# Dilated layer of a two-layer transformer trunk: query/key tiles of two of its three dilations transposed by DMA instead of TensorE

## The reference

```
DIL_PATTERNS = ((128, 1), (512, 4), (2048, 16))       # window, dilation

def dilated_mixer(a, cos, sin, w_in, w_o):
    proj = (a @ w_in).reshape(B, S, N_DIL, 3, H, DH)   # S = 256, H = 16 heads, DH = 64
    outs, lses = [], []
    for gi, (window, dil) in enumerate(DIL_PATTERNS):
        q = partial_rope(proj[:, :, gi, 0], cos, sin)
        k = partial_rope(proj[:, :, gi, 1], cos, sin)
        v = proj[:, :, gi, 2]
        o, lse = banded_attention(to_residue(q, dil)[:, :, :, None], to_residue(k, dil),
                                  to_residue(v, dil), window // dil)
        outs.append(from_residue(o[:, :, :, 0], B, dil))
        lses.append(from_residue(lse[:, :, :, 0], B, dil))
    alpha = jax.nn.softmax(jnp.stack(lses, axis=-1), axis=-1)
    o = jnp.einsum('bshn,bshnd->bshd', alpha.astype(a.dtype), jnp.stack(outs, axis=3))
    return o.reshape(B, S, H * DH) @ w_o
```

## Time and profile before

| | |
|---|---|
| median of 3 runs | 810.8 us (810.62 to 811.05) |
| the profiled execution, its own time | 810.76 us |
| its span, first to last instruction | 809.0 us |
| mean granted TensorE clock | 0.997 |
| PE busy / DVE busy / ACT busy / POOL busy | 798.6 / 528.5 / 457.5 / 102.2 us |
| the dilated layer in the trace | about 342 to 618 us |

### The profile page before, as it was taken

The page is one execution under the profiler, slowest core; times in us unless marked ns, Lnnn a source line. Parts: engine busy times, 40 slices in busy tenths (PEclk is TensorE's granted clock), DMA queues, the critical chain, the costliest instruction groups (busy, mean ns, idle before and its releaser), DMA issues.

```text
span 809.0 us, 11869 instructions
## 1 busy us (share of the span) xinstructions
PE 798.6 (99%) x4401; PEld 643.8 (80%) x4401; DVE 528.5 (65%) x1121; ACT 457.5 (57%) x879; POOL 102.2 (13%) x167
## 2 busy tenths in 40 slices
PE   9999999999999999999999999999999999999996
PEld 7877675788888888788888888888877888888885
DVE  6966969796565556697566665766668775655644
ACT  7836877765444444575555566555658554444431
POOL 1000005812212221000000000000000112222210
PEclk9999999999999999999999999999999999999998
DMA  9955211168886687658544535363424688678811
GB/s 318 351 184 200 86 54 53 59 189 241 242 212 191 191 238 216 188 198 269 157 157 153 160 121 192 105 208 105 157 88 172 191 248 224 173 197 236 236 21 52
DMA packets 128490, 142.24 MB, mean 176 GB/s; under 512 B 25856, under 2 KB 111920, under 8 KB 128304
## 3 DMA queue, kind: packets, MB, share of 16 engines
q1 hardware_dynamic: 107760, 132.53, 52.6%
q10 hardware_dynamic: 19680, 4.75, 3.6%
q0 software_dynamic: 992, 4.19, 1.4%
HBM read 134.64 MB, written 2.10 MB: 169 GB/s over the span
## 4 chain that ended last, share of the span: by engine, by line
PE 96%; DVE 2%; ACT 1%; issue 0%; POOL 0%; ACTq 0%; POOLq 0%
PE ps L1830 86%; PE ps L1839 6%; PE ps L2107 2%; PE ps L2080 2%; PE ps L2118 1%; PE ps L1892 1%; ACT junk L756 0%; DVE w_lo L1256 0%; ACT xd_hi L744 0%; ACT w_hi L735 0%; ACT probs_b L907 0%; DVE h L1580 0%; DVE h L1586 0%; DVE tmp L1584 0%; ACT p_t L922 0%
## 5 line engine op out<-in xcount | busy, mean ns | idle before, releaser
L1256 DVE TENSOR_TENSOR w_lo<-w_raw,w_hi 128x1024 fp32r<-128x1024 f32 x240 | 295.5, 1259 | 64.8 <-ACT w_hi L735 62.5
L735 ACT ACTIVATE w_hi<-w_raw 128x1024 fp32r<-128x1024 f32 x240 | 245.5, 1060 | 3.0 <-DMA w_raw<-in_ffn_w_gu 2.9
L1830 PE MATMUL ps<-w_hi,xt_hi 128*128 128x512 f32 x472 | 188.5, 401 | 0.3 <-ACT w_hi L735 0.3
L1830 PE MATMUL ps<-w_hi,xt_lo 128*128 128x512 f32 x472 | 183.5, 390 | 0.0
L1830 PE MATMUL ps<-w_lo,xt_hi 128*128 128x512 f32 x472 | 183.0, 390 | 0.0
L1830 PE MATMUL ps<-w_hi,xd_hi 128*128 128x512 f32 x288 | 117.4, 408 | 0.2 <-DVE w_lo L1256 0.2
L1830 PE MATMUL ps<-w_hi,xd_lo 128*128 128x512 f32 x288 | 113.2, 393 | 0.0
L1830 PE MATMUL ps<-w_lo,xd_hi 128*128 128x512 f32 x288 | 112.8, 392 | 0.0
L1830 PEld LDWEIGHTS ps<-w_hi,xt_hi 128*128 128x128 f32 x472 | 88.5, 188 | 25.0 <-issue 8.6
L1830 PEld LDWEIGHTS ps<-w_hi,xt_lo 128*128 128x128 f32 x472 | 88.6, 188 | 18.9
L1830 PEld LDWEIGHTS ps<-w_lo,xt_hi 128*128 128x128 f32 x472 | 88.7, 188 | 16.7 <-DVE w_lo L1256 0.3
(11 more groups left out here) (271 smaller groups left out, 984.9 us busy)
## 6 DMA issues: line engine op xcount, KB each, us to landing
w_raw<-in_ffn_w_gu SPq DMA_DIRECT2D x88, 512.0 KB, 5.6
w_raw<-in_dil_w_in SPq DMA_DIRECT2D x72, 512.0 KB, 4.6
w_raw<-in_ffn_w_down SPq DMA_DIRECT2D x44, 512.0 KB, 5.4
w_raw<-in_nsa_w_in SPq DMA_DIRECT2D x20, 512.0 KB, 7.3
w_raw<-in_nsa_w_o SPq DMA_DIRECT2D x8, 512.0 KB, 4.8
w_raw<-in_dil_w_o SPq DMA_DIRECT2D x8, 512.0 KB, 4.5
w_k<-in_nsa_cmp_wk SPq DMA_DIRECT2D x2, 1024.0 KB, 9.0
w_raw<-in_nsa_cmp_wv SPq DMA_DIRECT2D x2, 1024.0 KB, 11.5
```

The lines of the kernel that those rows point to most:

```text
L735: act.activation(w_hi[:, n.slot, c:c + 1024], w_raw[:, n.slot, c:c + 1024], ACT.Copy)\
L1256: dve.tensor_tensor(w_lo[:, n.slot, c:c + 1024], w_raw[:, n.slot, c:c + 1024], w_hi[:, n.slot, c:c + 1024].bitcast(F32), ALU.subtract)\
L1830: ins = pe.matmul(o, s, m, start=start, stop=stop, **kw)
```

## The change

Patterns 1 and 2 no longer go through PE. Their 16 tiles (four in each group, `BARS`) take the way of the FFN's hidden tiles: POOL splits `stage_dil` into planes (`split_qk`, 1024 columns of 16 bits), ACT issues a DMA transpose of them (`dil_planes`), POOL merges them into `qk_t` in class order (`merge_qk`, four copies of 256 elements a partition, six where pattern 2 has m = 0). The planes lie in the place of `h`, two buffers of each. So POOL saves `h` in two parts, ahead of its first split, and reads it back after the last merge. Every group now has the order 1, 2, 0: pattern 0 last, still turned on PE (`PE_TURNS`, 8 tiles). The factor -1/8 of the queries moves from the copies to the mask operation. PE's scores wait for the merges, do the parts of patterns 1 and 2 first, and then wait for `qk_lo`.

```diff
 def qk_order(g):
-    return (1, 2, 0) if g == 0 else (1, 0, 2)
+    return (1, 2, 0)
...
+BARS = [x for x in TILES if x.kind == QK and x.pat]
+PE_TURNS = [x for x in TILES if x.kind == QK and not x.pat]
...
+            def split_qk(x):
+                pool.wait_ge(roped[1], x.qk_no + 1)
+                pool.tensor_copy(view(planes_q, BARS.index(x) % 2 * 1024, [[512, 2], [1, 512]]),
+                                 halves_of(stage_dil[:, x.qk_no % 2, :])).then_inc(planes_ready, 1)
...
+            def merge_qk(x):
+                i, pos = BARS.index(x), qk_order(x.g).index(x.pat)
+                pool.wait_ge(planes_turned[i % 2], 16 * (xbar_of(0, FJ - 2, i % 2) + i // 2 + 1))
+                if x.g - (pos == 0) > 0:
+                    pool.wait_ge(scores[1], 8 * (x.g - (pos == 0)))
...
+                for plane in range(2):
+                    q = at + plane + 2 * 32 * x.m
+                    pool.tensor_copy(u16_at(whole, q, [[2 * S, 2], [2 * P, 2], [2 * 64, 2], [2, 32]]),
+                                     view(planes_qt, src + 512 * plane, [[P, 2], [1, 2], [2, 2], [4, 32]]))
...
+                    ins = pool.tensor_copy(u16_at(whole, k - 2 * shift, [[2 * S, 2], [2 * P, 2], [2, 64 - first]]),
+                                           view(planes_qt, k_src + 2 * first, [[P, 2], [1, 2], [2, 64 - first]]))
+                ins.then_inc(ht_merged, 1)
...
-                    pool.dma_start(h_rows.rearrange("(m p) c -> p m c", m=MT), h[:, :, :]).then_inc(h_saved, 16)
+                    save_h(0)
                     pool.wait_ge(h_saved, 16)
+                    save_h(1)
...
+                    for g in range(DIL_G):
+                        first, second, third, fourth = [x for x in BARS if x.g == g]
+                        split_qk(first)
+                        split_qk(second)
+                        merge_qk(first)
+                        split_qk(third)
+                        merge_qk(second)
+                        split_qk(fourth)
+                        merge_qk(third)
+                        merge_qk(fourth)
+                    pool.wait_ge(ht_merged, len(XBAR) + DIL_BARS)
                     pool.dma_start(h[:, :, :], h_rows.rearrange("(p m) c -> p m c", m=MT)).then_inc(h_permuted, 16)
...
+            def dil_planes(x):
+                if x not in BARS:
+                    return
+                i = BARS.index(x)
+                if i == 0:
+                    act.wait_ge(h_saved, 16 * MT)
...
+                act.wait_ge(planes_ready, bar_at(x) + 1)
+                act.dma_start_transpose(planes_qt[:, i % 2, :, :], planes_q[:, i % 2, :])\
+                   .then_inc(planes_turned[i % 2], 16)
...
-            dil_turn_out(TILES[0])
             dil_evac(TILES[1])
             h_squares(2, 1)
             split(n + 1)
             split(n + 2)
-            dil_turn_out(TILES[1])
+            dil_planes(TILES[0])
+            dil_planes(TILES[1])
             dil_evac(TILES[2])
             split(n + 3)
-            dil_turn_out(TILES[2])
+            dil_planes(TILES[2])
             for e in range(4, LAST_E):
...
                 dil_evac(TILES[e - 1])
...
                     split(n + k, (1,))
+                dil_planes(TILES[e - 1])
                 dil_turn_out(TILES[e - 1])
...
             def dil_turn(x):
-                if x.kind != QK:
+                if x not in PE_TURNS:
                     return
```

More of the change, by code:

```diff
@@ L119, with bar_at @@
 XBAR = [(1, 0), (1, 1)] + [(j, m) for j in range(2, FJ - 1) for m in range(MT)]
+DIL_BARS = 2 * MT * DIL_G
 def xbar_no(layer, j, m):
-    return len(XBAR) * layer + XBAR.index((j, m))
+    return (len(XBAR) + DIL_BARS) * layer + XBAR.index((j, m))
 def xbar_of(layer, j, m):
     tiles = [x for x in XBAR if x[1] == m]
-    return len(tiles) * layer + tiles.index((j, m)) + 1
+    return (len(tiles) + DIL_BARS // 2) * layer + tiles.index((j, m)) + 1
 TILES = dil_tiles()
 LAST_E = len(TILES)
-N_TURNS = sum(x.kind == QK for x in TILES)
-def firsts_until(qk_no):
-    return sum(x.kind == QK and x.pat == 0 and x.qk_no <= qk_no for x in TILES)
+BARS = [x for x in TILES if x.kind == QK and x.pat]
+PE_TURNS = [x for x in TILES if x.kind == QK and not x.pat]
+def bar_at(x):
+    return len(XBAR) + BARS.index(x)
 def pair_start(g, t):
@@ L661, in _ @@
                 p2 = mask_dil[rows, 0, 257 - cls:DIL_N:2]
[L662 removed]
+                link(pool.affine_select(out=p1, in_=p1, compare_op=ALU.is_ge, fill=NEG / SCALE,
                                         base=0, pattern=[[-1, 64]], channel_multiplier=1))
[L664 removed]
+                link(pool.memset(p2, NEG / SCALE))
                 for d in range(0, 64, 4):
@@ L1119, in dil_turn_out @@
             def dil_turn_out(x):
-                if x.kind != QK:
+                if x not in PE_TURNS:
                     return
[L1122 to L1125, removed]
+                no = PE_TURNS.index(x)
+                act.wait_ge(turned[1], no + 1)
+                at = qk_slot(x.g, 0) * 4 * S
+                src = (2 + no % 2) * 512
@@ L1126, in dil_turn_out @@
                 for hp in range(2):
[L1127 to L1137, removed]
@@ L1447, in cmp_probs, with mask_part @@
                    .then_inc(pc_ready, 1)
-            def mask_part(dst, w, c, n, mask, least):
-                return dve.tensor_tensor_reduce(out=dst, in0=bank(score_bank(w), c, n), in1=mask, scale=1.0,
+            def mask_part(dst, w, c, n, mask, least, scale=1.0):
+                return dve.tensor_tensor_reduce(out=dst, in0=bank(score_bank(w), c, n), in1=mask, scale=scale,
                                                 scalar=INF, op0=ALU.add, op1=ALU.min, accum_out=least)
@@ L2410, in dil_turn @@
             def dil_turn(x):
-                if x.kind != QK:
+                if x not in PE_TURNS:
                     return
+                no = PE_TURNS.index(x)
                 pe.wait_ge(roped[1], x.qk_no + 1)
-                if x.qk_no >= 2:
-                    pe.wait_ge(turn_out[1], x.qk_no - 1)
-                    if firsts_until(x.qk_no - 2):
-                        pe.wait_ge(qk_lo_ready, firsts_until(x.qk_no - 2))
+                if no >= 2:
+                    pe.wait_ge(qk_lo_ready, no - 1)
                 for k in range(4):
-                    ins = turn(2 + x.qk_no % 2, k, stage_dil[:, x.qk_no % 2, P * k:P * k + P])
+                    ins = turn(2 + no % 2, k, stage_dil[:, x.qk_no % 2, P * k:P * k + P])
                 ins.then_inc(turned[1], 1)
@@ L2425, in head, with first_q, first_k @@
                             p0=DH * (j % 2), n=DH)
-            def first_hi(g, t, j, c, n):
-                return view(qk_hi, (qk_slot(g, 0) * 4 + 2 * t + j // 2) * S + c, [[1, n]], p0=DH * (j % 2), n=DH)
-            def first_lo(t, j, c, n):
-                return view(qk_lo[2 * t + j // 2], c, [[1, n]], p0=DH * (j % 2), n=DH)
+            def first_q(g, j, m):
+                rows, cols = slice(DH * (j % 2), DH * (j % 2) + DH), slice(m * P, (m + 1) * P)
+                return qk_hi[rows, qk_slot(g, 0), j // 2, cols], qk_lo[j // 2][rows, cols]
+            def first_k(g, j):
+                rows = slice(DH * (j % 2), DH * (j % 2) + DH)
+                return qk_hi[rows, qk_slot(g, 0), 2 + j // 2, :], qk_lo[2 + j // 2][rows, :]
             def dil_scores(g, t):
```

73 lines of the change are left out of this document (47 added, 26 removed).

## The result

The changed kernel takes **806.2 us** (median of 4 runs, 805.99 to 806.67), the kernel before, on the same chip, 810.7 us (4 runs, 810.25 to 811.05). The ratio is 0.9945, 95% interval 0.9931 to 0.9959: faster by 4.5 us, where the prediction had no change. It fell into the range of the rival "the chain is short".

A forecast was written before the change was run, and what follows sets the result against it. The prediction took PE, busy 99% of the span, as the bound; 810.76 - 5.8 (turns saved) + 4.5 (first tiles' stall) + 1.6 (groups 1 and 3) = 811.1 us, range 806.0 to 815.5.

The forecast's parts named there:

- the chain is short: Rival: landing 4.5 to 6 us or an issue of 1.2, stall 0 to 2, 805.0 to 808.8 us; chance 0.26.
- First issue: 359.4: Start of the dilated layer: ACT issues the first tile's transposes at 359.4, about 0.6 us before its last queued operation ends.
- the stall of 4.5 us: First four tiles of the layer: PE waits for the rotated tile from 374.5 to 379.0, 4.5 us.
- The landing: Time from ACT's transpose issue to POOL's merge at the layer's beginning: 8.3 us, bounds 2.4 and 11.9.
- The issue: ACT's cost of issuing one tile's transposes, 1024 columns: 1.95 us, between 1.21 and 2.4.
- The merge: POOL's four merge copies of 256 a tile, at 0.45 us each: 1.9 us with their gaps.
- PE's saving: 16 tiles no longer turned on PE, 0.36 us each: 5.8 us saved if nothing else waits.
- Groups 1 and 3: Rounds 13, 16 and twins: transpose issue delays ACT's copy of turned probabilities, PE waits 0.4 us four times, 1.6 us.
- collision rival: POOL and DVE hold each other up on the first chain and ahead of probabilities: 817.7 us, middle 815; chance 0.22.
- start chain: First four DMA tiles, one projection apart, forming a serial chain through ACT and POOL that stalls PE by 4.5 us.
- The `p_t` mechanism: In four rounds PE waits for ACT's copy of turned probabilities behind a transpose issue, 0.4 us each.
- What costs nothing: Scores after merges, group 2, the read of `h`, the last tile's `qk_lo` and ACT's load: no cost expected.

The follow-up runs named there:

- e2_late_issue: The changed kernel with ACT's first transpose issue of the layer waiting until its engine has ended the four weight halves ahead; 812.0 us.
- e4_turns_back: The changed kernel with four PE transposes of a constant, read by nothing, at each of the 16 places where tiles were turned before; 813.2 us.
- e1_norm_first: The changed kernel with DVE normalising the first head's probabilities ahead of the rotation of the q/k tile instead of behind it; 804.5 us.
- e3_two_issues: The changed kernel with each tile's transposes issued as two of 512 columns instead of one of 1024; 817.1 us.
- e8_split_waits: The changed kernel with POOL's split waiting for DVE's normalising product in the rounds where it follows the rotation, DVE's order kept; 811.2 us.
- e7_order_only: The kernel before with only the changed kernel's order of dilations and place of the last tile's low parts, all tiles turned on PE; 810.6 us.
- e5_fill_wait: e2_late_issue with 26 PE transposes of a constant ahead of the wait for `rs_perm`; 812.6 us.
- e6_mid_issue: The changed kernel with ACT's first transposes waiting for two of the four weight halves only; 808.8 us.

## Why the prediction was wrong

**The step that failed** is "ACT issues about 0.6 us before its last operation ends, as 656.13 against 656.74 shows. First issue: 359.4." In the earlier trace rows both issues did come 0.6 and 0.8 us before the end of the queued weight halves, but what they waited for was POOL's split, which the same trace has ending at 656.10 and 664.39, 0.03 us ahead of each issue; I took a coincidence for a rule.

```profile
655.49 0.61 POOL L683 COPY planes<-hs 128x512 uint16<-128x512 uint16 x1 [0.32 <-DVE hs L1594]
...
663.65 0.74 POOL L683 COPY planes<-hs 128x512 uint16<-128x512 uint16 x1 [4.28 <-DVE hs L1594]
```

An issue in ACT's program waits for its semaphores and for the sequencer, not for the engine to end what is queued ahead. So it came at 356.0, 3.4 us earlier than forecast, and the stall of 4.5 us was at most 0.1. e2_late_issue puts the late issue alone back: +5.8 us.

**The landing** (L = 8.3) was 3.4 us, because the early issue met idle DMA engines. It is for the greater part the same mistake: issued late it was 6.1 to 6.4, still 2 us under the forecast. The stretch's DMA share of 1.09 in the earlier trace rows was read rightly, but DMA was idle beyond 356, with a share of 0.00 up to 358, and that the first tile could be ahead of the refills was not asked:

```profile
356.00:358.00 2.00, 2.00 (x11) 1.62 (x10) 1.41 (x8) 2.00 (x4) 0.15 (x1) 1.00 0.00 0
```

**The issue** (i = 1.95) was 1.25. The fit through a plain DMA of 0.41 us had no ground: the issue of a transpose costs 1.21 to 1.25 us whether it carries 512 or 1024 columns.

**Two terms were missing that work the other way.** The merge was put at 1.9 us and took 4.1 in e2_late_issue, 3.3 in the changed kernel (359.42 to 362.7), for copies that ran beside DVE. And a stall was priced at its length, when the clock's fall behind it cost nearly as much again. With the first issue at 359.9 the kernel does lose 5.8 us, against 4.5 predicted: that this is near is luck, too long a landing and issue standing in for the merge and the clock.

**PE's saving** (5.8) was too small: 6.7 by e4_turns_back. I took the price between two weight products for nearly all tiles; 6 of 16 stand behind turned probabilities, at 0.44.

**Groups 1 and 3** (1.6, on ACT's `p_t`) measured 1.85 us in just these four rounds, from another cause: DVE's product behind POOL's split. That is the collision rival's mechanism; its price was 3 us for the groups, and the 6.7 + 3 us that it had for the start chain didn't come. The `p_t` mechanism was about 0.15 us away (e1_norm_first), and appears in e3_two_issues and e8_split_waits.

**What costs nothing** held: the order (e7_order_only), group 2, the scores, the read of `h`, the low parts.

The sum with measured terms: -6.7 + 0.1 + 1.85 = -4.75, against -4.73 in the layer. The rival "the chain is short" gave the right range and part of the reason (a fast landing, an issue that doesn't grow); its condition was one step earlier, the moment of the issue. Two bounds were loose besides: that rival's own terms (0 to 2 us of stall, next to nothing later) end at 807.0, not 808.8, and the collision's middle is 815 in one place and 815.5 in the range.

## What to carry to other kernels

When a DMA is issued from ACT's queue, as here, find the semaphore it waits for, and don't add the engine work written ahead of it. Then look at what the DMA engines hold at that moment: 1.8 us later, this transfer stood behind a refill of some 0.9 MB and took twice as long, and ordering the refill behind it gave all of that back. Where a slack is a few tenths, ask for every two operations that start running side by side on DVE and POOL which of them somebody waits for, and let the other one take the collision.

## What was not expected of the hardware

- Behind four waits of PE of 2.0 to 3.2 us (e2_late_issue, e3_two_issues, e5_fill_wait, e6_mid_issue), the granted clock fell to its lower level and five to eleven instructions took 427 instead of 228 ns. In e8_split_waits four equal waits of 1.6 us were followed by a slow stretch only once, which began 2.6 us behind the end of the first. Which waits bring it about stays open.
- The issue of a tile's transposes took 1.25 us as a rule, but 3.47 us in e6_mid_issue and 2.5 in e2_late_issue, for the second tile, while the first tile's packets stood behind the refills. An issue can so be held up by the fill of its own queue, it seems; this wasn't tested.
- A POOL copy of 4 columns took 1.17 us beside a weight half of DVE, and 0.20 where no weight half ran, in the changed kernel.
